# Neighbourhood scores on the two row halves in pairs, and latent attention's values by four heads, in a two-block transformer kernel

## The reference

```python
for l in range(DEPTH):
    h = rms_norm(x, g_mix[l])
    proj = h @ w_in[l]
    c_q, c_kv, k_r, qkv_b, qkv_c, gate_logits = jnp.split(proj, IN_SPLITS, axis=-1)
    y_a = mla_mixer(c_q, c_kv, k_r, g_q[l], g_kv[l], w_uq[l], w_ukv[l])      # latent, 8 heads
    ...
    y_b = dilated_mixer(q_b, k_b, qkv_b[:, :, 2])                            # dilated, 12 heads
    ...
    y_c = neighbourhood_mixer(qkv_c[:, :, 0], qkv_c[:, :, 1], qkv_c[:, :, 2], rpb[l])   # 8 heads
    ...
    x = x + merged @ w_o[l]
    h = rms_norm(x, g_ffn[l])
    x = x + (jax.nn.silu(h @ w1[l]) * (h @ w3[l])) @ w2[l]
```

```python
s = jnp.einsum('bchd,bcnhd->bhcn', q_row, kg, preferred_element_type=jnp.float32) * scale
s = s + bias.astype(jnp.float32)[None]
p = jax.nn.softmax(s, axis=-1).astype(v.dtype)
return jnp.einsum('bhcn,bcnhd->bchd', p, vg)
```

## Time and profile before

| | us |
|---|---|
| median of 3 runs | 2605.05 |
| lowest and highest | 2604.26, 2609.89 |
| profiled execution | 2613.94 |
| its span in the trace | 2612.1 |
| TensorE busy | 2524.0 (97% of the span) |
| POOL busy | 1936.3 (74%) |
| VectorE busy | 1116.2 (43%) |
| ScalarE busy | 684.1 (26%) |

### The profile page before, as it was taken

How to read it: one execution, slowest core, us unless ns; L and a number is a source line. 1 busy time by engine, 2 the same in 40 slices (tenths; PEclk the granted TensorE clock), 3 DMA queues, 4 the chain that set the end, 5 groups by cost and what they waited for, 6 DMA issues and landing times.

```text
span 2612.1 us, 38097 instructions
## 1 busy us (share of the span) xinstructions
PE 2524.0 (97%) x13034; PEld 2019.4 (77%) x13034; DVE 1116.2 (43%) x1618; ACT 684.1 (26%) x1300; POOL 1936.3 (74%) x1567
## 2 busy tenths in 40 slices
PE   7999999999999999999999999999999999999998
PEld 6776777777788888777687777788887777778776
DVE  5556443224222225546625224322225338650775
ACT  3445233112201012536314111210002115231341
POOL 6777855989889898867873899898998573447704
PEclk9999999999999999999999999999999999989998
DMA  4233421233233323223420223333332121112201
GB/s 136 86 97 98 154 73 53 86 92 99 90 98 96 97 93 92 89 89 96 163 89 29 92 87 99 95 97 96 97 96 93 57 81 57 41 35 89 75 23 64
DMA packets 67569, 226.62 MB, mean 87 GB/s; under 512 B 7552, under 2 KB 16256, under 8 KB 66944
## 3 DMA queue, kind: packets, MB, share of 16 engines
q1 hardware_dynamic: 66016, 221.32, 26.8%
q10 hardware_dynamic: 1440, 3.79, 0.4%
HBM read 222.99 MB, written 2.10 MB: 86 GB/s over the span
## 4 chain that ended last, share of the span: by engine, by line
POOL 36%; PE 32%; issue 20%; DVE 5%; DMA 3%; POOLq 2%; ACT 0%; SPq 0%; DVEq 0%; ACTq 0%
POOL whi L469 18%; POOL wlo L472 12%; PE ps L565 8%; PE ps L567 8%; PE ps L566 8%; POOL raw L488 3%; POOL ada_acc L490 3%; DMA raw<-w_gate 2%; DMA raw<-w_abc 1%; PE ps L674 1%; PE ps L643 1%; PE ps L599 1%; PE ps L953 1%; DVE q_parts L1883 1%; POOLq L471 1%
## 5 line engine op out<-in xcount | busy, mean ns | idle before, releaser
L469 POOL TENSOR_TENSOR whi<-raw,one 128x512 fp32r<-128x512 f32 (+3 forms) x732 | 794.5, 1085 | 546.7 <-PE ps L567 471.6
L472 POOL TENSOR_TENSOR wlo<-raw,whi 128x512 fp32r<-128x512 f32 (+3 forms) x732 | 952.9, 1302 | 57.3
L565 PE MATMUL ps<-h,whi 128*128 128x512 f32 x1984 | 795.7, 401 | 34.5 <-POOL wlo L472 16.5
L567 PE MATMUL ps<-h,wlo 128*128 128x512 f32 x1984 | 780.6, 393 | 0.0
L566 PE MATMUL ps<-h,whi 128*128 128x512 f32 x1984 | 780.3, 393 | 0.0
L565 PEld LDWEIGHTS ps<-h,whi 128*128 128x128 f32 x1984 | 376.7, 190 | 137.2 <-POOL wlo L472 29.7
L567 PEld LDWEIGHTS ps<-h,wlo 128*128 128x128 f32 x1984 | 376.0, 190 | 81.9
L566 PEld LDWEIGHTS ps<-h,whi 128*128 128x128 f32 x1984 | 376.6, 190 | 79.2 <-issue 2.4
L565 PE MATMUL ps<-y,whi 128*128 128x512 f32 x640 | 250.9, 392 | 0.6 <-DVE y L1805 0.6
L567 PE MATMUL ps<-y,wlo 128*128 128x512 f32 x640 | 249.0, 389 | 0.0
L566 PE MATMUL ps<-y,whi 128*128 128x512 f32 x640 | 249.0, 389 | 0.0
(11 more groups left out here) (286 smaller groups left out, 3012.3 us busy)
## 6 DMA issues: line engine op xcount, KB each, us to landing
raw<-w SPq DMA_DIRECT2D x120, 512.0 KB, 3.4
raw<-w_abc SPq DMA_DIRECT2D x68, 512.0 KB, 3.5
raw<-w_ada SPq DMA_DIRECT2D x48, 512.0 KB, 3.5
raw<-w_gate SPq DMA_DIRECT2D x48, 512.0 KB, 3.5
raw<-w_in SPq DMA_DIRECT2D x44, 512.0 KB, 3.5
raw<-w_pac SPq DMA_DIRECT2D x16, 512.0 KB, 3.5
raw<-w_o SPq DMA_DIRECT2D x16, 512.0 KB, 3.5
raw<-w_out SPq DMA_DIRECT2D x16, 512.0 KB, 3.5
```

What stands on the lines that cost most here:

```text
L469: pool.tensor_tensor(whi[:, s, r], raw[:, s, r], one[:, 0:1].to_broadcast([P, cols // 2]), ALU.mult).then_inc(hi_made, 1)
L472: pool.tensor_tensor(wlo[:, s, r], raw[:, s, r], whi[:, s, r].bitcast(F32), ALU.subtract).then_inc(made, 1)
L565: nc.tensor.matmul(out, whi[:, s, w], moving[:, c, :], start=(c == 0), stop=False)
L567: last = nc.tensor.matmul(out, wlo[:, s, w], moving[:, c, :], start=False, stop=(c == n - 1))
```

## The change

Three things are changed, and each of the three streams with them.

1. *Neighbourhood attention.* The keys lie as the queries do, two heads in a tile, so `kc` has 4 tiles and not 8; the memsets and their semaphore go, and VectorE writes a key tile with one operation of 128 rows. A score is a matmul over the 64 rows of its head's half, for even heads the lower and for odd heads the upper one. Scores are given in pairs (`paired`): behind the transposes of an odd head i come the scores of i + 3 and i + 4, and behind those of an even head none. ScalarE takes the exponentials two heads ahead and not three. Ahead of the loop TensorE waits for the bank of the last but one key unit; the score of head 4 waits no more.
2. *Latent attention.* `group=4`: behind the transposes of every fourth head come the values of four heads. `pt` gets a fourth buffer, `pt_a`, in a free part of y. The reciprocals move in front of the last four heads' values, and VectorE and ScalarE take their parts of them one head earlier.
3. *All attentions.* In `values` the wait for `pt_ready` stands behind the reciprocals and not in front of them.

```diff
-        kc_ = at("kc", [P, C_HEADS, T], hd + 4 * TILE)
+        kc_ = at("kc", [P, C_TILES, T], hd + 4 * TILE)
...
+        slots_a = [*tmp, at("pt_a", [P, T], y_at + 12 * TILE)[:]]
...
+                evicted = (0,) if group == 2 else (2, 3)
...
-                    elif chunks <= 4 and i >= 2 and i % 2 == 0:
+                    elif chunks <= 4 and i >= 2 and i % group in evicted:
                         pe.wait_ge(pt_ready, pt_0 + i - 1)
...
-                    pe.wait_ge(pt_ready, pt_0 + i + 2)
...
-                    if hh == n_heads - 2:
+                    if hh == n_heads - group:
                         reciprocals(qb)
+                    pe.wait_ge(pt_ready, pt_0 + i + 2)
...
                         turn(i)
-                        if i + ahead < n:
+                        if paired:
+                            for k in (i + ahead - 1, i + ahead):
+                                if i % 2 == 1 and k < n:
+                                    score(k)
+                        elif i + ahead < n:
                             score(i + ahead)
-                    if i >= 2 and i % 2 == 0:
+                    if group == 2 and i >= 2 and i % 2 == 0:
                         values(i - 2)
+                    elif group == 4 and i % 4 == 3:
+                        values(i - 3)
+                        values(i - 1)
...
                 def c_scores(b, hh, bank):
-                    if b == 0 and hh in (4, 6):
+                    if (b, hh) == (0, 6):
                         pe.wait_ge(bank_free[hh // 2 - 2], free_n[hh // 2 - 2].now() + 1)
-                    return nc.tensor.matmul(ps[bank][:, 0:C_WIN], qc_[:, hh // 2, b * P:(b + 1) * P],
-                                            kc_[:, hh, C_START[b]:C_START[b] + C_WIN], start=True, stop=True)
+                    r = slice(HD * (hh % 2), HD * (hh % 2) + HD)
+                    return nc.tensor.matmul(ps[bank][:, 0:C_WIN], qc_[r, hh // 2, b * P:(b + 1) * P],
+                                            kc_[r, hh // 2, C_START[b]:C_START[b] + C_WIN], start=True, stop=True)
...
-                ahead = max(2, len(ring) - 1)
+                ahead = 2
...
-                    if i > 0 and i % n_heads == 0:
+                    if (i > 0 and i % n_heads == 0) if group == 2 else (i < n and i % n_heads == n_heads - 1):
...
-                nc.vector.memset(kc_[HD:P, 0::2, :], 0.0)
-                nc.vector.memset(kc_[0:HD, 1::2, :], 0.0).then_inc(kc_zeroed, 1)
...
-                        for half in range(2):
-                            r = slice(HD * half, HD * half + HD)
-                            to, frm = by_column(kc_[r, 2 * (first + t) + half, :], ps[t][r, :])
-                            _, by = by_column(kc_[r, 2 * (first + t) + half, :], rsb[r, :])
-                            last = nc.vector.tensor_tensor(to, frm, by, ALU.mult)
-                        last.then_inc(bank_free[t], 1)
+                        to, frm = by_column(kc_[:, first + t, :], ps[t][:])
+                        _, by = by_column(kc_[:, first + t, :], rsb[:])
+                        nc.vector.tensor_tensor(to, frm, by, ALU.mult).then_inc(bank_free[t], 1)
```

More of the change, by code:

```diff
@@ L620, in attention @@
             def attention(n_heads, scores, value, chunks, ring, slots, banks, o_banks, r_bank, o_read=None, between=None,
-                          ready=None):
+                          group=2, ready=None, paired=False):
                 n = NQB * n_heads
@@ L905, in _ @@
                 attention(C_HEADS, c_scores, c_value, 2, ring_c, slots_c, (2, 3, 4, 5), (7,), 1,
-                          between=c_qk_rest, ready=v_read)
+                          between=c_qk_rest, ready=v_read, paired=True)
                 def branch(at, n):
@@ L1507, in add_x, with attention @@
                 free_n[first].next()
-            def attention(n_heads, cols, maximum, move_pt, y_out, ring, slots, o_banks, out, r_bank, gated=False, between=None):
+            def attention(n_heads, cols, maximum, move_pt, y_out, ring, slots, o_banks, out, r_bank, gated=False, between=None,
+                          group=2):
                 n = NQB * n_heads
@@ L1528, in attention @@
                     qb = i // n_heads - 1
-                    if block_end:
-                        dve.wait_ge(p_ready, p_0 + i)
-                        nc.vector.reciprocal(rden[:, 0:n_heads], den[:, qb % 2, 0:n_heads]).then_inc(rden_ready, 1)
+                    last = i if group == 4 else i - 1
+                    if 0 <= last < n and last % n_heads == n_heads - 1:
+                        dve.wait_ge(p_ready, p_0 + last + 1)
+                        nc.vector.reciprocal(rden[:, 0:n_heads], den[:, last // n_heads % 2, 0:n_heads]).then_inc(rden_ready, 1)
                     if i < n and move_pt:
                         dve.wait_ge(t_done, t_n.next())
-                        nc.vector.tensor_copy(slots[i % 3][:, 0:cols], ps[(6, 0)[i % 2]][:, 0:cols]).then_inc(pt_ready, 1)
+                        nc.vector.tensor_copy(slots[i % len(slots)][:, 0:cols], ps[(6, 0)[i % 2]][:, 0:cols]).then_inc(pt_ready, 1)
                     if i + len(ring) < n:
```

23 lines of the change are left out of this document (11 added, 12 removed).

## The result

| | before | after |
|---|---|---|
| median of the runs, us | 2606.88 (20 runs, 2601.91 to 2612.74) | 2617.81 (20 runs, 2610.36 to 2626.36) |
| profiled execution, its span | 2612.1 | 2624.6 |

The account below looks back on a forecast made before the run. TensorE's own instructions and the few waits between them bound both attentions. 2 x (5.5 neighbourhood - 1.6 latent - 0.44 reciprocals) = +6.9 us takes the median from 2605.05 to 2611.9, range 2602 to 2618.5.

Parts of the forecast that it names:

- forecast case: Whole kernel: between 2 and 9 us slower than before, given a chance of 0.58.
- rival 1: Neighbourhood attention: paired scores on row halves don't overlap and take 0.87 us; +12 us, 2617; chance 0.12.
- The period of a block: Neighbourhood attention: late scores and product lengthen a block from 9.60 to 12.2 us, +2.6 for each full period.
- The start and the front: Neighbourhood attention: shorter wait for the last keys, and faster scores ahead of the last projections, -0.5 us each a layer.
- The steady pair: Neighbourhood attention: TensorE's work for two heads between block ends goes from 2.04 to 1.98 us, gaining 0.06.
- The trip: Neighbourhood attention: TensorE's change into the row-half tile form and back costs 0.37 us for each pair of scores.
- rival 3: Neighbourhood attention comes out even as ScalarE and VectorE catch up at block ends; -4 us, 2601; chance 0.12.
- rival 4: Neighbourhood attention: row-half trips are hidden, a pair takes 1.61 us on TensorE; -7 us, 2598; chance 0.10.
- The +8 a layer: Neighbourhood attention's slower bound: without any overlap each pair of scores is 0.43 us longer, the layer +8 us.
- The cap by POOL: Behind latent attention: the first projection waits for POOL to cut its weights, so only 1.6 us a layer are kept.
- Rival 2: Latent attention gives nothing because VectorE can't follow four heads in a row; +10 us, 2615; chance 0.08.
- Reciprocals ahead of the wait: End of dilated attention: TensorE's reciprocal passes move into an idle wait, 0.44 us a layer kept; nothing between blocks.

Follow-up runs that it names:

- b3_both: After, with VectorE's reciprocal ahead of the maxima of heads 10 and 11 and the block product ahead of head 12's maximum: 2594.61 us, 0.9948 of before.
- a4_full_rows: After, with before's zero-padded keys, so every score in neighbourhood attention is a matmul of 128 rows, still in pairs: 2614.30 us, 1.0030 of before.
- a1_latent: Before, with only latent attention's part of the change and the reciprocals ahead of the wait for a head's copy: 2602.42 us, 0.9983 of before.
- a2_neigh: Before, with only neighbourhood attention's part: keys on row halves, paired scores, exponentials two ahead: 2624.49 us, 1.0064 of before.
- b1: After, with VectorE's reciprocal ahead of the maxima of heads 10 and 11 in neighbourhood attention alone: 2602.60 us, 0.9987 of before.
- c2: a1_latent, with the four scores ahead of the last projections on row halves and VectorE's reciprocal ahead of the maxima of heads 10 and 11: 2595.26 us, 0.9963 of before.
- c4: a4_full_rows, with the reciprocal ahead of the maxima of heads 10 and 11 and the product ahead of head 12's maximum: 2594.07 us, 0.9957 of before.
- c5: b3_both unchanged, timed again on another chip beside c2 and c4: 2596.13 us, 0.9959 of before.
- b2: After, with VectorE's block product ahead of the maximum of head 12 in neighbourhood attention alone, reciprocal left in place: 2610.06 us, 1.0015 of before.
- d1_after_again: After, unchanged, timed and profiled a second time: 2618.69 us, 1.0043 of before.
- a3_filled: After, with eleven useless identity transposes ahead of TensorE's wait for the reciprocals in neighbourhood attention alone: 2615.39 us, 1.0026 of before.
- b4_halves_alone: Before, with row halves alone, one 64-row score behind each head's transposes and exponentials three ahead: 2613.97 us, 1.0030 of before.

## Why the prediction was right or wrong

**Direction and forecast case**: slower, for the stated reason, the late scores and the two waits at a block's end; but its size is not the forecast's. The prediction gave its own case +2 to +9, and +10.9 lies above that. The time is inside the whole range only because the range was drawn up to 2618.5 for rival 1, scores that don't overlap, and they do. That is luck: after's second set of runs, at 2618.69, lies just outside.

**The waits.** At a block end the four moments from the pair to R came within 0.01 us, and in a block without a fall so did R to V(6), to S(12), to V(8) and to the next pair (0.92, 1.83, 4.15, 5.11, against 0.92, 1.82, 4.17, 5.12). Of what would show it right, three signs came: R idle 1.6 on rden, V(8) idle 1.3 on the product, the two heads' scores 7 ns apart in start. The fourth, about 45 us for the attention, did not: the profiled stretches are 48.20 and 49.49, and 46.14 in the second execution.

**The period of a block**: 12.2 forecast, 12.33 in each block without a fall. The last 9.7 forecast, 9.65 measured. The start and the front, 0.5 less each in the forecast, are 0.57 (9.83 to 9.26 from the first T to R) and 0.55 less. Neighbourhood attention without falls is 45.04, +6.1 a layer against a forecast of +6.0 without the front.

**The steady pair**: 1.98 forecast, 1.96 in b3_both (its pairs at 377.27 and 379.23). The trip, 0.37 from dilated attention, is 0.35 here. The overlap, taken from V's pairs, holds. Rival 1, no overlap, is out; rival 3, a block end that comes out even, and rival 4, the trip hidden, too. "The steady pair gains 0.06" holds (2.04 to 1.96) for pairs that wait for nothing, and fails as the worth of the row halves, for which a4's expectation took it: a4_full_rows has blocks of 11.77, so on this order they cost 0.56 a block, since the trip also delays the scores that VectorE waits for. The +8 a layer that the prediction set for pairs without overlap is not worked out there: 16 pairs of 0.43 on top of 5.5 would be 12.4 if no wait took them up, so the upper end of the range was too low for its own rival. No run tests it.

**The step that failed**: the period of 12.2 us takes TensorE's work behind the two waits at the lengths of before. The prediction added a wait of 1.5 us and one of 1.75 to a block and noted that the granted clock was 1.00, and never asked whether it would stay: the clock's term was put at nothing. Each fall costs 1.1 to 1.6 us in after, and there were five and two of six in two profiled executions. Without falls the two layers give 2 x (6.1 - 0.55 + 0.13 - 1.07 - 0.61) = 8.0, the forecast 6.9. The 2.9 that are left to the measured 10.9 would be two falls of that size in a typical run. The timed runs, which show only their mean clock, bear this out. A straight line through the 81 runs of before that stand beside the experiments (mean clock 0.9869) falls by 2.1 us for each 0.001 of clock, with a scatter of 1.2. After's 20 runs have a mean clock of 0.9854, which that line prices at 3.1 us, and lie 7.4 us above it, close to the 8.0. That is an estimate, and it does not say where in the kernel the clock was lost.

**Latent attention**: the last two heads' V starts at 287.8 in after, 291.9 on the clock of before (the attentions start 4.1 us later there), inside the forecast's 291.0 to 292.5. TensorE's own gain is 2.1 us (62.52 to 60.39 from the first T to V's last pass, in every kernel with groups of four), inside 1.6 to 3.1. The cap by POOL was there, but is no fixed number: over 22 layers of eleven such kernels the first projection came between 0.20 and 1.66 us behind V's last pass, 0.91 in the mean, where before has 0.20; why it varies was not followed up. So 1.4 us are kept in the mean, forecast 1.6. Rival 2 is out.

**Reciprocals ahead of the wait**: 0.44 forecast for dilated attention's tail, 0.61 measured. R took its change of form along into the wait. "Nothing elsewhere" was wrong at one place: the last block end of neighbourhood attention, where before's R stands behind a copy by ScalarE and not behind rden. That is 0.54 a layer (8.42 to 7.88 in a1_latent); I had looked at an inner block end and taken it for all.

**The faster side**: rival 4 asked for trips below 0.1 us. What was faster than before in the end came another way, by two places in VectorE's queue, which the prediction itself names as the reason for both waits.

## What to carry to other kernels

When a change adds waits of TensorE, ask for two prices: the wait, and the work behind it at half clock, which in a block that fell was up to as much again; and take the second from several executions, since one profile can hold five falls and the next two. When a wait is traced to a place in another engine's queue, look whether the awaited step has to stand there: in b3_both the reciprocal runs ahead of two maxima and R finds it ready. And before a layout is taken over for its streaming time, weigh it in the order it will run in: full rows and row halves ended level, 9.31 and 9.33 us a block, when the order was mended, and before's own order with one step moved did as well.

## What the runs showed of the hardware

The clock falls at a block end in some executions and not in others, with the same rows around it: five of six and two of six in the same kernel, six of six in a2_neigh, one of six where either the rden wait was filled or V(8)'s wait removed, none of six where R's wait was removed (b1, b3, c2, c4, c5) or the scores had 128 rows in pairs (a4). These are single executions, and b2's timed runs have the clock of a kernel with more falls than its profile. A fall began at R's start or shortly behind it in after's first execution, and behind V(8) in d1_after_again and a3_filled. What decides the single case stays open. A fall cost 1.4 to 1.7 us where it began at R, 1.1 in d1's two blocks, and 0.4 in a3_filled's.

The changes between the tile forms that these kernels have (128x128 to 64x128 and back, 128x64 to 128x128, and 64x128 straight to 128x64) cost 0.15 to 0.20 us each in b4_halves_alone. Two fp32 scores on the two row halves start 7 ns apart and run beside each other: the transposes behind them start 0.63 us after the pair, and 0.62 after a single head's score.
